# Fourteen of sixteen weight groups of an up projection as seven half-block products in place of eight

## The chip, the cores and the metric

The kernel runs on one core of a Trainium2 chip. The metric is the device time of one execution in microseconds. Before the change it is 2390.11 us, the median of 3 runs (2389.84 to 2390.34).

## What is computed

One layer of a decoder with a prompt group of 2048 tokens and a sample group of 64 tokens, model width 1024: an input projection, sliding-window attention and mLSTM heads, an output projection, then the channel MLP with hidden width 4096. The change is in the MLP alone:

```python
def channel_mlp(x, g, w_up, w_down):
    h = rmsnorm(x, g)
    u = jnp.maximum(jnp.einsum('btd,df->btf', h, w_up), 0)
    return jnp.einsum('btf,fd->btd', u * u, w_down)
```

All data are float32.

## The kernel before, in words

**Quarters.** The tokens are worked in four quarters of 512 (TQ); the last takes the 64 sample tokens too (576, TMAX). Each quarter runs weight units in a fixed order: 6 units F and 4 units T of the input projection (the attention and the mLSTM run between them), 4 units O of the output projection, and 32 units M of the MLP, from unit number U_M = 14 to UNITS - 1 = 45. An M unit is half a chunk: a chunk U is 512 hidden columns of w_up (two units of 256), a chunk D the same 512 rows of w_down (two units of 512 output columns). The order of chunks is U0, U1, D0, U2, D1, ... U7, D6, D7 (lines 160 to 162): two up units, two down units, and so on.

**Exactness by parts.** TensorE multiplies in a reduced float format (float32r), so each operand is kept as a high part and a low part (the rest), and each product is three matmuls: high x high, high x low, low x high (gemm, lines 2057 to 2069). High parts are made by ScalarE (a copy with rounding), low parts by VectorE (the source minus the high part). For weights these are split_act (ScalarE, line 702 with the norm's gain as a scale, line 705 without) and split_vec (VectorE, lines 1173 and 1177), from the pieces w_raw that SyncE loads (512 KB, three buffers); a unit has two pieces and there are two buffers of split weights, w_hi and w_lo.

**An up unit** is 2 tiles of 128 hidden columns, each over 8 blocks of 128 of the model width. The hidden column tile is the weight operand and the 512 tokens are the moving operand; in the last quarter the tokens go as 256 and 320. ScalarE takes relu out of PSUM (line 1055) and squares it rounded to the high part (line 1057); VectorE squares it and subtracts for the low part (line 1181). Up units use PSUM banks 0 to 3, down units banks 4 to 7, where VectorE adds each result to x1 (line 1181).

**Queues.** Every engine runs its own instructions in the order in which the code writes them, and waits on semaphores. In the MLP each engine walks the same units by a function step. The walks of ScalarE and VectorE prepare unit u + 1 during unit u.

**Around the ends.** Before the MLP, norm_tile scales a token tile, TensorE transposes it (turn), and high_tile and low_tile split it into a_hi and a_lo. The first unit's second half waits for all low parts. In the last down units of a quarter the next quarter's tokens are prepared: stats_ahead (ScalarE), scale_ahead (VectorE, lines 1515 to 1537) in units UNITS - 4 and UNITS - 2, turn_ahead (TensorE, transposes at line 2115, ahead of the unit's matmuls), high_ahead (ScalarE) and take_ahead (VectorE, line 1563) in units UNITS - 3 and UNITS - 1. In VectorE's step these calls stand ahead of the unit's own additions. TensorE's next quarter starts with a wait for all of take_ahead.

Of the kernel before, what the change touches and what calls it, by code (L numbers as in the profile page):

```python
# [6 lines left out]
F32 = mybir.dt.float32  # L7
# [7 lines left out]
P = 128  # L15
# [40 lines left out]
WMAX = KT * TMW  # L56

# [14 lines left out]


# [75 lines left out]

def up_order(u, NN):  # L150
# [7 lines left out]


MLP_HEAD = [("U", 0)]  # L160
MLP_BODY = 3
MLP_TAIL = [("U", NC - 1), ("D", NC - 2), ("D", NC - 1)]


def hymba_layer(nc, x_prompt, x_sample, cache_k_win, cache_v_win, state_C, state_n, state_m, rel_bias,
# [5 lines left out]
    with ctx:  # L171
        def sb(name, shape, dt=F32, where=ctx):
            return where.enter_context(nc.sbuf_tensor(name, shape, dt))


        raw = [sb(f"w_raw{s}", [P, WMAX // 2]) for s in range(RAW)]
        w_hi = [sb(f"w_hi{b}", [P, WMAX], F32R) for b in range(UNIT_BUFS)]
        w_lo = [sb(f"w_lo{b}", [P, WMAX], F32R) for b in range(UNIT_BUFS)]

# [3 lines left out]
        sample_parts, sample_again = slice(TQ, TMAX + NS), slice(TMAX, TMAX + NS)  # L183
        x1 = sb("x1", [P, BLK + 1, D])
        square = sb("square", [P, 4, P])
        ident, triu, ntriu, cmask = (square[:, i, :] for i in range(4))
        ones = sb("ones", [P, P], F32R)
        bias = sb("bias", [P, H, 2 * P])
# [4 lines left out]
        bgate = sb("bgate", [P, 2 * HM])  # L193
        kk = sb("kk", [P, 2, P + TMAX])
# [7 lines left out]
        kwin = bias[:, 0, 0:KVH * DH]  # L202
# [26 lines left out]
        oms = sb("oms", [NS, HM, DV], where=phase)  # L229
        phase.close()  # L230
# [3 lines left out]
        relu = sb("relu", [P, 2, TMAX], where=phase)  # L234
        usq = sb("usq", [P, 2, TMAX], where=phase)
# [34 lines left out]
        def signal(name, per, first=0, extra=0):  # L270
# [8 lines left out]
        w_high = signal("w_high", PIECES)  # L279
        w_split = signal("w_split", PIECES, RAW)  # L280
# [24 lines left out]
        up_out, up_read = signal("up_out", 4 * NC, 1), signal("up_read", 4 * NC, 1)  # L305
# [24 lines left out]
        (s_in, s_bias0, s_ck, s_msk, s_cs, s_rows, s_rowsok, s_rrows, s_cols, s_ccols, s_kout, s_kok, s_sout, s_nmax, s_sum,  # L330
         s_esa, s_esok, s_mout, s_ib, s_dadd, s_d, s_tout, s_k2, s_st, s_q, s_kw, s_h, s_hsq, s_hn, s_hout,
         s_p_ok, s_ptout, s_ptv, s_pta, s_o, s_os, s_on, s_osq, s_osum, s_oss, s_kwm, s_c, s_cok, s_new, s_res, s_nst,
         s_mix_vec, s_mix_act, s_split, s_nin, s_nout, s_ncopy, s_step) = (
            signal("s_" + n, 0) for n in (
                "in bias0 ck msk cs rows rowsok rrows cols ccols kout kok sout nmax sum "
                "esa esok mout ib dadd d tout k2 st q kw h hsq hn hout "
                "p_ok ptout ptv pta o os on osq osum oss kwm c cok new res nst "
                "mix_vec mix_act split nin nout ncopy step").split())
# [19 lines left out]
        def y_tile_last(j):  # L358

            return usq[:, :, :].rearrange("p a t -> p (a t)")[:, 0:D] if j == BLK else y_tile(j)  # L360
# [6 lines left out]
        def unit_shape(u):  # L367
            kind, i, w = unit_of(u)
            return (4, 512) if kind == "O" or kind == "M" and mlp_unit(i)[0] == "D" else (KT, w)

        def mlp_unit(m):

            order = MLP_HEAD + [(k, c) for i in range(MLP_BODY) for k, c in (("U", 2 * i + 1), ("D", 2 * i), ("U", 2 * i + 2), ("D", 2 * i + 1))] + MLP_TAIL
            kind, c = order[m // 2]
            return kind, c, m % 2

        chunk_parity = {}
        kinds = MLP_HEAD + [(k, c) for i in range(MLP_BODY) for k, c in (("U", 2 * i + 1), ("D", 2 * i), ("U", 2 * i + 2), ("D", 2 * i + 1))] + MLP_TAIL
        for n, (kind, c) in enumerate(kinds):
            chunk_parity[U_M + 2 * n] = chunk_parity[U_M + 2 * n + 1] = c % 2  # L380
# [2283 lines left out]
```

## Time and profile before

| | us |
|---|---|
| median of 3 runs | 2390.11 |
| span of the profiled execution | 2388.1 |
| TensorE busy (matmuls) | 2362.5 |
| TensorE weight loads busy | 2016.6 |
| VectorE busy | 1377.4 |
| ScalarE busy | 963.6 |
| GpSimd busy | 79.3 |

The span is the profiled execution from its first instruction to its last. Busy times are summed durations of an engine's instructions with overlaps counted once; weight loads run beside matmuls. A matmul's duration contains its way through the array, so the distance between the starts of two matmuls is shorter than the duration of one.

### The profile page before, as it was taken

How to read it: one execution, taken by the hardware profiler on the slowest of the kernel's cores; microseconds unless marked ns; L12 is line 12 of the kernel's file. 1: busy time of each engine (PE TensorE's matmuls, PEld its weight loads, DVE VectorE, ACT ScalarE, POOL GpSimd, SP SyncE). 2: the span in 40 equal slices, each digit the busy share in tenths (PEclk: the TensorE clock that was granted, in tenths of full speed). 3: DMA queues.
4: the chain of work that ended last, by engine and by line, in shares of the span. 5: the costliest groups of instructions: out<-in, count | busy, mean ns of one | idle time of the engine just before them, and what ended most of it. 6: DMA issues, size and time to landing. Idle time of an engine off the chain costs nothing.

```text
span 2388.1 us, 33521 instructions
## 1 busy us (share of the span) xinstructions
PE 2362.5 (99%) x13086; PEld 2016.6 (84%) x13086; DVE 1377.4 (58%) x3162; ACT 963.6 (40%) x2050; POOL 79.3 (3%) x136
## 2 busy tenths in 40 slices
PE   9999999999999999999999999999999999999998
PEld 8988888888897888888998788888888879889996
DVE  4478554456378654455456854554656785555555
ACT  4445433334345533334333543333434454333332
POOL 3000000000000000000000210000010000000000
PEclk9999999999999999999999999999999999999999
DMA  6212323333511223324421233223444122222221
GB/s 193 79 45 90 96 97 98 96 109 106 170 55 54 81 96 97 96 90 132 147 80 37 68 99 97 90 96 97 133 124 133 45 67 88 77 84 80 88 80 66
DMA packets 175402, 224.28 MB, mean 94 GB/s; under 512 B 15107, under 2 KB 126308, under 8 KB 175228
## 3 DMA queue, kind: packets, MB, share of 16 engines
q1 hardware_dynamic: 162636, 192.63, 25.8%
q10 hardware_dynamic: 6448, 19.40, 2.3%
q0 software_dynamic: 6160, 10.11, 1.6%
q8 instruction: 103, 1.69, 0.3%
q14 instruction: 55, 0.45, 0.1%
HBM read 210.72 MB, written 12.60 MB: 94 GB/s over the span
## 4 chain that ended last, share of the span: by engine, by line
PE 95%; DVE 4%; ACT 1%; issue 1%; DVEq 0%; ACTq 0%
PE ps L2066 28%; PE ps L2068 28%; PE ps L2067 27%; PE ps L2077 2%; PE ps L2207 2%; PE ps L2187 1%; PE ps L2196 1%; PE ps L2253 1%; PE ps L2256 1%; DVE w_lo L1177 1%; PE ps L2103 0%; PE ps L2596 0%; PE ps L2115 0%; PE ps L2232 0%; DVE w_lo L1173 0%
## 5 line engine op out<-in xcount | busy, mean ns | idle before, releaser
L2068 PE MATMUL ps<-a_hi,w_lo 128*128 128x512 f32 (+2 forms) x1672 | 583.9, 349 | 0.0
L2066 PE MATMUL ps<-a_hi,w_hi 128*128 128x512 f32 (+2 forms) x1672 | 582.1, 348 | 0.6 <-DVE a_lo L1181 0.2
L2067 PE MATMUL ps<-a_lo,w_hi 128*128 128x512 f32 (+2 forms) x1672 | 582.0, 348 | 0.0
L702 ACT ACTIVATE w_hi<-w_raw,gains 128x256 fp32r<-128x256 f32 (+1 forms) x576 | 253.2, 521 | 411.3 <-PE ps L2068 290.6
L2066 PE MATMUL ps<-w_hi,u_all 128*128 128x512 f32 x1024 | 403.8, 394 | 0.0
L2068 PE MATMUL ps<-w_hi,u_all 128*128 128x512 f32 x1024 | 403.8, 394 | 0.0
L2067 PE MATMUL ps<-w_lo,u_all 128*128 128x512 f32 x1024 | 401.3, 392 | 0.0
L2066 PEld LDWEIGHTS ps<-a_hi,w_hi 128*128 128x128 f32 x1672 | 315.8, 189 | 43.1 <-DVE a_lo L1181 1.4
L2067 PEld LDWEIGHTS ps<-a_lo,w_hi 128*128 128x128 f32 x1672 | 314.0, 188 | 40.9
L2068 PEld LDWEIGHTS ps<-a_hi,w_lo 128*128 128x128 f32 x1672 | 314.2, 188 | 39.4
L1181 DVE TENSOR_TENSOR x<-x,ps 128x512 f32<-128x512 f32 (+1 forms) x288 | 196.5, 686 | 259.8 <-PE ps L2068 241.9
L1177 DVE TENSOR_TENSOR w_lo<-w_raw,w_hi 128x1024 fp32r<-128x1024 f32 (+2 forms) x208 | 242.9, 1182 | 119.0 <-ACT w_hi L705 119.0
L1173 DVE SCALAR_TENSOR_TENSOR w_lo<-w_raw,gains,w_hi 128x256 fp32r<-128x256 f32 (+1 forms) x576 | 257.7, 510 | 58.0 <-ACT w_hi L702 58.0
L1181 DVE TENSOR_TENSOR usq<-relu 128x512 f32<-128x512 f32 (+2 forms) x160 | 95.8, 599 | 321.9 <-ACT relu L1055 321.1
L2066 PE MATMUL ps<-w_hi,a_hi 128*128 128x290 f32 (+1 forms) x768 | 262.0, 341 | 0.3 <-DVE w_lo L1177 0.3
L2067 PE MATMUL ps<-w_lo,a_hi 128*128 128x290 f32 (+1 forms) x768 | 252.7, 329 | 0.0
L2068 PE MATMUL ps<-w_hi,a_lo 128*128 128x290 f32 (+1 forms) x768 | 252.5, 329 | 0.0
L1055 ACT ACTIVATE relu<-ps 128x512 f32<-128x512 f32 (+2 forms) x160 | 83.4, 521 | 401.7 <-PE ps L2068 316.6
L705 ACT ACTIVATE w_hi<-w_raw 128x1024 fp32r<-128x1024 f32 (+2 forms) x208 | 201.7, 1017 | 106.7 <-PE ps L2068 75.7
L2068 PEld LDWEIGHTS ps<-w_hi,u_all 128*128 128x128 f32 x1024 | 192.2, 188 | 45.3
L2067 PEld LDWEIGHTS ps<-w_lo,u_all 128*128 128x128 f32 x1024 | 192.4, 188 | 44.7
L2066 PEld LDWEIGHTS ps<-w_hi,u_all 128*128 128x128 f32 x1024 | 192.2, 188 | 43.2
(378 smaller groups left out, 2336.1 us busy)
## 6 DMA issues: line engine op xcount, KB each, us to landing
w_raw<-in_w_up_dram SPq DMA_DIRECT2D x128, 512.0 KB, 3.7
w_raw<-in_w_down_dram SPq DMA_DIRECT2D x128, 512.0 KB, 3.5
w_raw<-in_w_out_dram SPq DMA_DIRECT2D x32, 512.0 KB, 3.5
w_raw<-in_w_in_dram SPq DMA_DIRECT2D x24, 580.0 KB, 4.9
w_raw<-in_w_in_dram SPq DMA_DIRECT2D x22, 512.0 KB, 3.7
w_raw<-in_w_in_dram SPq DMA_DIRECT2D x32, 256.0 KB, 2.9
wide<-in_x_prompt_dram ACTq DMA_DIRECT2D x12, 512.0 KB, 4.6
x<-in_x_prompt_dram ACTq DMA_DIRECT2D x9, 512.0 KB, 6.2
```

The costliest lines, as they stand in the source:

```text
L702: ins = eng.activation(w_hi[b][:, k * n:(k + 1) * n][:, s], src[:, s], ACT.Copy, scale=gain[:, a:a + 1])
L705: eng.activation(w_hi[b][:, k * n:(k + 1) * n], src[:, 0:n], ACT.Copy).then_inc(w_high.sem, 1)
L1055: eng.activation(relu[:, l % 2, 0:w], ps[(l + 2) % 4][:, 0:w], ACT.Relu).then_inc(up_read.sem, 1)
L1173: ins = eng.scalar_tensor_tensor(w_lo[b][:, k * n:(k + 1) * n][:, s], raw[raw_of(q, p)][:, s], gain[:, a:a + 1], w_hi[b][:, k * n:(k + 1) ...
L1177: eng.tensor_tensor(w_lo[b][:, k * n:(k + 1) * n], raw[raw_of(q, p)][:, 0:n], w_hi[b][:, k * n:(k + 1) * n].bitcast(F32), ALU.subtract).th ...
L1181: return eng.tensor_tensor(out, a, b, op)
L2066: eng.matmul(out, lh, rh, start=(k == ks[0]), stop=False)
L2067: eng.matmul(out, lh, rl, start=False, stop=False)
L2068: ins = eng.matmul(out, ll, rh, start=False, stop=(k == last))
L2077: ins = eng.matmul(out, lhs(k), right, start=(k == ks[0] and part == 0), stop=(k == ks[-1] and part == 1))
L2187: ins = eng.matmul(ps[b][:, at:at + 2 * P], zT[rs, h // 2, cs], kk[rs, int(g != par), j * P:j * P + 2 * P], start=True, stop=True)
L2207: ins = eng.matmul(values_at(g)[:, h, :], PT[:, 2 * g + half, h * P:(h + 1) * P], vv[:, j + half, g, :], start=(half == 0), stop=(half == 1))
```

## The change

The up projection of 14 of the 16 up units of each quarter (all but the first two) is computed by seven products. The unit's weights are cut into four blocks, by half of the model width (512 each) and by tile of 128 hidden columns; the tokens' activations into four blocks, by the same halves of the model width and by token half (256). With four sums of weight blocks (S1 to S4) and four sums of activation blocks (T1 to T4), seven products of a 128-column block over 512 give the four results by additions (Winograd's form of Strassen's scheme). Each product is still three matmuls per 128 of the width: 84 matmuls of 256 columns in place of 48 of 512. In the last quarter the 64 sample tokens ride with one token half, in four of the seven products.

- The activations' sums are made once per quarter (x_sums, 4 VectorE operations; then t_high_part on ScalarE and t_low_part on VectorE, four each). For them the normed activations are kept in float32: take_tile writes them from PSUM to SBUF times the norm's gain, and high_tile and low_tile read that. The gain is no longer in the weight splits.
- The weights' sums are made in each unit (sum_forms, 4 VectorE operations), then seven high parts (high_form, ScalarE) and seven low parts (low_form, VectorE), each 128x512, into a ring of nine slots in place of the two buffers; the plain M units use four slots each.
- The products stand in PSUM banks 0 to 3 in turn. ScalarE copies the first to SBUF (take_copy), VectorE adds the others up (take_sum 0 to 6). ScalarE then does relu, square and the rounding copy (square_up), VectorE the low part (low_sum).
- Buffers overlap otherwise, for room: the bias table of the attention lies where T parts lie in the MLP and is loaded again in every quarter (bias_again, GpSimd queue).
- The calls scale_ahead and take_ahead stand at the end of VectorE's step, behind the unit's additions.

The core of the diff:

```diff
+FORM = 512
+RING = 9
+N_PLAIN = 2
+FORMS_OF = "A11 A12 S1 S2 S4 S3 A22".split()
...
+        def ring_free(eng, q, u, f):
...
+            at = ring_at(u) + f
+            if at < RING:
+                eng.wait_ge(op_out.sem, op_out.at(q, op_end(NT, 2 if at < 4 else 3)))
+                return
+            v, g = RING_USER[at - RING]
+            kind, c, half = mlp_unit(v)
+            if seven(v) is not None:
+                eng.wait_ge(m_done.sem, m_done.at(q, 7 * seven(v) + g + 1))
+            elif kind == "U":
+                eng.wait_ge(up_out.sem, up_out.at(q, 2 * NN * (half + 1)))
+            else:
+                eng.wait_ge(dn_out.sem, dn_out.at(q, 2 * NT * c + NT * (half + 1)))
...
+        def product_bank(at, n):
+
+            return ps[(7 * at + n + 2) % 4]
```

On GpSimd's queue, and on ScalarE (step and its helpers):

```diff
+                if q < QI:
+                    pool.wait_ge(m_done.sem, m_done.at(q, 7 * N_SEVEN))
+                    bias_again()
...
+            def high_form(q, u, f):
+
+                name = FORMS_OF[f]
+                if name[0] == "S":
+                    eng.wait_ge(f_sum.sem, f_sum.at(q, 4 * seven(u) + {"S1": 1, "S3": 2, "S2": 3, "S4": 4}[name]))
+                else:
+                    landed(eng, q, 2 * u + int(name[2]) - 1)
+                ring_free(eng, q, u, f)
+                eng.activation(form_at(w_hi_all, u, f), form_src(q, u, name), ACT.Copy).then_inc(f_high.sem, 1)
...
+                def square_up(u, phi):
...
+                    eng.wait_ge(c_add.sem, c_add.at(q, 7 * at + 4 + 3 * phi))
+                    eng.activation(c_at[phi], c_at[phi], ACT.Relu).then_inc(u_rel.sem, 1)
+                    eng.wait_ge(u_rel.sem, u_rel.at(q, 2 * at + phi + 1))
+                    eng.activation(c_at[phi], c_at[phi], ACT.Square).then_inc(u_sq.sem, 1)
...
+                    eng.activation(u_hi[c % 2][:, half * 2 + phi, 0:T], c_at[phi], ACT.Copy).then_inc(u_high.sem, 1)
...
+                    if seven(u) is not None:
+                        if seven(u) == 0:
+                            t_high_part("T3")
+                        if before is not None:
+                            square_up(before, 1)
+                        take_copy(u)
+                        next_part(0)
+                        next_part(1)
+                        next_part(2)
+                        next_part(3)
+                        square_up(u, 0)
```

On VectorE:

```diff
+            def take_tile(q, NT, k):
...
+                    gain = gains[:, 2, 4 * m:4 * m + 4].unsqueeze(2).broadcast_to([P, 4, R])
+                    tt(x_flat(NT > BLK)[m][:, :, n * P:n * P + R], ps[4 + (2 * k + m) % 4][:, 0:4 * R].rearrange("p (k t) -> p k t", k=4), gain, ALU.mult).then_inc(xf_ok.sem, 1)
...
+                    if before is not None:
+                        take_sum(before, 6)
+                    if seven(u) is not None:
+                        if seven(u) == 0:
+                            t_low_part(3)
+                        next_part(0)
+                        if before is not None:
+                            low_sum(before, 0)
+                        next_part(1)
+                        take_sum(u, 0)
+                        if before is not None:
+                            low_sum(before, 1)
+                        next_part(2)
+                        take_sum(u, 1)
+                        take_sum(u, 2)
+                        next_part(3)
+                        take_sum(u, 3)
+                        next_part(4)
+                        take_sum(u, 4)
+                        take_sum(u, 5)
+                        next_part(5)
+                    elif kind == "U":
+                        if half:
+                            next_part(0)
+                            next_part(1)
+                            next_part(2)
+                        else:
+                            next_part(0)
+                            next_part(3)
+                            x_sums()
+                            t_low_part(0)
+                            t_low_part(1)
                         for n, (t, s) in enumerate(up_order(u, NN)):
...
+                            low_up(u, t, off, w, half * 2 * NN + n + 1)
...
+                        next_part(5)
+                    if u == UNITS - 4 and not last:
+                        scale_ahead(q + 1, 0)
+                    if u == UNITS - 3 and not last:
+                        take_ahead(q + 1, 0)
+                    if u == UNITS - 2 and not last:
+                        scale_ahead(q + 1, 1)
+                    if u == UNITS - 1 and not last:
+                        take_ahead(q + 1, 1)
```

Here next_part(0) and (1) are two weight sums each for the next unit, next_part(2) to (5) the low parts of forms 0 and 1, 2 and 3, 4, 5 and 6; for a plain next unit next_part(0) and (3) are its two splits. On TensorE:

```diff
+                    bank_free(0, 2)
+                    product(u, 0, ws, b11)
+                    bank_free(1, 4)
+                    product(u, 1, ws, b21)
+                    bank_free(2, 6)
...
+                    product(u, 2, ws, turned_part("T1"))
+                    bank_free(3, 7)
...
+                    product(u, 3, HT, turned_part("T2"))
+                    eng.wait_ge(cp_ok.sem, cp_ok.at(q, at + 1))
+                    product(u, 4, HT, b22)
+                    eng.wait_ge(c_add.sem, c_add.at(q, 7 * at + 1))
...
+                    product(u, 5, HT, turned_part("T3"))
+                    eng.wait_ge(c_add.sem, c_add.at(q, 7 * at + 3))
+                    product(u, 6, ws, turned_part("T4"))
```

bank_free(n, count) waits until VectorE has done that many takes of the unit before.

## Rows read from the trace of the kernel before

**Rows 1.** The page: span, then busy time of each engine, share, instructions.
```profile
span 2388.1 us, 33521 instructions
PE 2362.5 (99%) x13086; PEld 2016.6 (84%) x13086; DVE 1377.4 (58%) x3162; ACT 963.6 (40%) x2050; POOL 79.3 (3%) x136
```
**Rows 2.** Stage windows: us, busy of PE, PEld, DVE, ACT, POOL, clock, DMA.
```profile
238.00:594.00 356.00, 356.00 (x1558) 289.76 (x1557) 186.39 (x323) 137.07 (x262) 0.00 (x0) 1.00 0.32 101
...
1982.00:2366.00 384.00, 384.00 (x2286) 346.68 (x2285) 204.35 (x390) 130.44 (x274) 0.00 (x0) 1.00 0.25 79
```
**Rows 3.** Groups by line and shape, weight loads: busy, mean ns of one.
```profile
L2066 PEld LDWEIGHTS ps<-a_hi,w_hi 128*128 128x128 f32 x1672 | 315.8, 189 | 43.1 <-DVE a_lo L1181 1.4 <-DVE w_lo L1173 1.1 <-issue 1.0
```
**Rows 4.** Timeline of PE, 512 columns: start us, duration, instruction.
```profile
400.10 0.39 PE L2067 MATMUL ps<-a_lo,w_hi 128*128 128x512 f32 x1
...
404.27 0.39 PE L2067 MATMUL ps<-a_lo,w_hi 128*128 128x512 f32 x1
...
404.73 0.39 PE L2066 MATMUL ps<-w_hi,u_all 128*128 128x512 f32 x1
```
**Rows 5.** Timeline of PE, 256 columns, in two units.
```profile
1982.03 0.28 PE L2067 MATMUL ps<-a_lo,w_hi 128*128 128x256 f32 x1
...
1984.07 0.28 PE L2067 MATMUL ps<-a_lo,w_hi 128*128 128x256 f32 x1
...
2301.00 0.28 PE L2067 MATMUL ps<-a_lo,w_hi 128*128 128x256 f32 x1
...
2302.43 0.28 PE L2067 MATMUL ps<-a_lo,w_hi 128*128 128x256 f32 x1
```
**Rows 6.** Timeline of PE, 320 columns.
```profile
1979.89 0.31 PE L2067 MATMUL ps<-a_lo,w_hi 128*128 128x320 f32 x1
...
1981.62 0.31 PE L2067 MATMUL ps<-a_lo,w_hi 128*128 128x320 f32 x1
```
**Rows 7.** Groups by line and shape, DVE.
```profile
L1177 DVE TENSOR_TENSOR w_lo<-w_raw,w_hi 128x1024 fp32r<-128x1024 f32 x152 | 185.2, 1222 | 34.9 <-ACT w_hi L705 34.9
L1181 DVE TENSOR_TENSOR x<-x,ps 128x512 f32<-128x512 f32 x256 | 174.6, 686 | 242.4 <-PE ps L2068 241.9
...
L1181 DVE TENSOR_TENSOR ST<-ps,DT 128x256 f32<-128x256 f32 x32 | 12.1, 420 | 4.7 <-ACT DT L708 4.3
```
**Rows 8.** Timeline of DVE in an up unit.
```profile
400.78 0.69 DVE L1181 TENSOR_TENSOR u_all<-usq,u_all 128x512 fp32r<-128x512 f32 x1
401.38 1.22 DVE L1177 TENSOR_TENSOR w_lo<-w_raw,w_hi 128x1024 fp32r<-128x1024 f32 x1
```
**Rows 9.** Timeline of ACT behind an up unit.
```profile
404.93 0.60 ACT L1055 ACTIVATE relu<-ps 128x512 f32<-128x512 f32 x1 [4.26 <-PE ps L2068]
405.56 0.63 ACT L1057 ACTIVATE u_all<-relu 128x512 fp32r<-128x512 f32 x1
```
**Rows 10.** Timeline of DVE at the end of the first quarter.
```profile
566.61 0.17 DVE L1515 TENSOR_SCALAR st<-st 128x2 f32<-128x2 f32 x1 [2.00 <-ACT PT L793]
...
567.84 1.42 DVE L1537 TENSOR_SCALAR wide<-wide,st 128x1024 f32<-128x1024 f32 x2
...
576.45 4.23 DVE L1563 SCALAR_TENSOR_TENSOR a_lo<-ps,gains,a_hi 128x128 fp32r<-128x128 f32 x16 [0.75 <-ACT a_hi L837]
...
586.27 0.69 DVE L1181 TENSOR_TENSOR x<-x,ps 128x512 f32<-128x512 f32 x1 [2.11 <-PE ps L2068]
```
**Rows 11.** Timeline of PE there.
```profile
573.13 1.91 PE L2115 MATMUL ps<-square,wide 128*128 128x128 f32 x16
...
586.07 0.40 PE L2066 MATMUL ps<-a_hi,w_hi 128*128 128x512 f32 x1
```
**Rows 12.** Timeline of DVE at the start of the first MLP.
```profile
230.96 1.29 DVE L1181 TENSOR_TENSOR a_lo<-ps,a_hi 128x512 fp32r<-128x512 f32 x2 [0.86 <-ACT a_hi L735]
```
**Rows 13.** Timeline of PE there.
```profile
227.33 1.09 PE L2103 MATMUL ps<-square,wide 128*128 128x128 f32 x8 [0.63 <-DVE wide L1243]
...
232.31 0.39 PE L2066 MATMUL ps<-a_hi,w_hi 128*128 128x256 f32 x1
```

More of the change, by code:

```diff
@@ L71, in dmas_of, with mlp_unit, seven, plain_before @@
     return 3 if u == U_T else 1
+MLP_HEAD = [("U", 0)]
+MLP_BODY = 3
+MLP_TAIL = [("U", NC - 1), ("D", NC - 2), ("D", NC - 1)]
+MLP_ORDER = MLP_HEAD + [(k, c) for i in range(MLP_BODY) for k, c in (("U", 2 * i + 1), ("D", 2 * i), ("U", 2 * i + 2), ("D", 2 * i + 1))] + MLP_TAIL
+def mlp_unit(u):
+    kind, c = MLP_ORDER[(u - U_M) // 2]
+    return kind, c, (u - U_M) % 2
+def seven(u):
+    if not U_M <= u < UNITS:
+        return None
+    kind, c, half = mlp_unit(u)
+    return 2 * c + half - N_PLAIN if kind == "U" and 2 * c + half >= N_PLAIN else None
+N_SEVEN = sum(seven(u) is not None for u in range(UNITS))
+FORMS_OF = "A11 A12 S1 S2 S4 S3 A22".split()
+def plain_before(u):
+    return 2 * sum(seven(v) is None for v in range(u))
+PLAIN = plain_before(UNITS)
+def ring_at(u):
+    return sum(4 if seven(v) is None else 7 for v in range(U_M, u))
+RING_USER = [(u, f) for u in range(U_M, UNITS) for f in range(4 if seven(u) is None else 7)]
 def raw_of(q, p):
@@ L368, in unit_shape @@
             kind, i, w = unit_of(u)
[L369 to L380, printed above, removed]
+            return (4, 512) if kind == "O" or kind == "M" and mlp_unit(u)[0] == "D" else (KT, w)
         block = ctx.enter_context(nc.Block())
@@ L1988, in step @@
-                            eng.wait_ge(u_sq.sem, u_sq.at(q, o + 1))
-                            low(l, o, t, off, w)
-                            if n == NN - 1 and not end and u != U_M:
-                                split_vec(eng, nq, nu, 1, i)
+                            low_up(u, t, off, w, half * 2 * NN + n + 1)
+                        if half:
+                            for n in (3, 4, 5):
+                                next_part(n)
+                        else:
+                            t_low_part(2)
@@ L2561, in quarter, with t_at @@
                     eng.wait_ge(op_read.sem, op_read.at(q, 4 * NT))
-                def step(kind, c, half, u, i):
+                ws = staging(last)[0]
+                t_hi, t_lo = ({name: parts[i] for name, parts in t_forms(last).items()} for i in range(2))
+                def t_at(name, k, w):
+                    if name == "T2":
+                        return t_hi[name][:, k // 2, k % 2, 0:w], t_lo[name][:, k, 0:w]
+                    return t_hi[name][:, k, 0:w], t_lo[name][:, k, 0:w]
@@ new lines, in product @@
+                def product(u, f, w, right):
+                    eng.wait_ge(f_split.sem, f_split.at(q, 7 * seven(u) + f + 1))
+                    hi, lo = form_at(w_hi_all, u, f), form_at(w_lo_all, u, f)
+                    out = product_bank(seven(u), f)[:, 0:w]
+                    for k in range(4):
+                        rh, rl = right(k, w)
+                        eng.matmul(out, hi[:, k, :], rh, start=(k == 0), stop=False)
+                        eng.matmul(out, hi[:, k, :], rl, start=False, stop=False)
+                        ins = eng.matmul(out, lo[:, k, :], rh, start=False, stop=(k == 3))
+                    ins.then_inc(m_done.sem, 1)
```

641 lines of the change are left out of this document (444 added, 197 removed).

## The prediction

> **What bounds the kernel now.** I read the busy times of the page first: TensorE is busy 2362.5 of 2388.1 us, VectorE 1377.4, ScalarE 963.6 [rows 1]. Then the busy time by stage: in the MLP of the first quarter (238 to 594 us) TensorE is busy for all 356 us, VectorE for 186, ScalarE for 137; in that of the last quarter 384, 204 and 130 of 384 [rows 2]. So a matmul taken out there is time taken out, as long as the other two engines feed TensorE; VectorE has 170 us of room in a quarter's MLP. The granted clock is 1.00 in both stretches [rows 2], the upper level of 2.4 GHz, with TensorE never idle before; I leave the clock out of the sum.
>
> The duration of a matmul in the trace overlaps its neighbours, so I take its price from starts. At 512 columns, 18 matmuls from 400.10 to 404.27 us: 0.2317 us each [rows 4]. At 256 columns there are two rates: 18 from 1982.03 to 1984.07, 0.1133 each, and 12 from 2301.00 to 2302.43, 0.1192 each [rows 5]; in the last quarter they alternate from unit to unit. At 320 columns 12 from 1979.89 to 1981.62: 0.1442 [rows 6]. Each brings its own weight load, 189 ns long [rows 3], and the 256-column ones still start every 0.113 to 0.119 us, so loads are pipelined beside matmuls and half-width products cost half.
>
> The Trainium skill (TensorE: Matmul & The Clock Gate, Back-to-back issue gap) gives 262 cycles for 256 columns and 518 for 512, but adds that spacing in a stream is set by weight load and matmul together. By its isolated figures a plain unit would be 48 x 0.216 = 10.4 us and seven products 84 x 0.109 = 9.2, an estimate that saves 1.2 us where the rows below save 1.36; its warning about the load would speak against 84 small matmuls, but the starts of rows 5 show no such cost.
>
> **What TensorE saves.** A plain unit (256 hidden columns) is 2 tiles x 8 k x 3 passes = 48 matmuls of 512 columns, 11.12 us. Seven products are 7 x 4 k x 3 = 84 matmuls of 256 columns: 9.52 us at the fast rate, 10.01 at the slow one. The new weight slots lie elsewhere in memory, so I can't tell which; I take the middle, 0.1162, or 9.76 us. It saves 1.36 us (1.11 to 1.60), times 14 units times 3 quarters: 57.1 us (46.6 to 67.2). In the last quarter a plain unit is 48 of 256 and 48 of 320 columns, 5.58 + 6.92 = 12.50 us; four of its seven products stay 320 wide and three are 256: 6.92 + 36 x 0.1162 = 11.10. It saves 1.40 (1.2 to 1.5), times 14: 19.6 us. **Together 76.7 us, 64 to 88.**
>
> **What VectorE and ScalarE must do for it.** To prepare one seven-unit, VectorE makes 4 sums and 7 low parts of 128x512; to finish one it takes 7 partial sums of 128x256 out of PSUM and makes 2 low parts of 128x512. A 128x512 operation lasts 686 ns, a 128x256 one 420, a 128x1024 one 1222 [rows 7], but one that depends on nothing just before starts 0.60 us after a 128x512 one (400.78 to 401.38 [rows 8]); so 0.60, about 0.33 (420 less the same 90) and 1.13. ScalarE's steps are 0.60 and 0.63 [rows 9]; each reader of PSUM starts 0.20 us after the next group's first matmul (404.73 to 404.93 [rows 4, 9]).
>
> The units go up, up, down, down. In a first up unit (start 0, end 9.76) VectorE comes out of the down unit late: last addition at 0.2, two low parts whose slots came free only when that unit ended, done at 2.0. Then 4 sums (4.5), first take (4.9), two low parts (6.1), second and third take (6.9), two low parts (8.1), fourth (8.4), a low part (9.0), fifth and sixth (9.7), two low parts (10.9), seventh (11.3). TensorE's seventh product, at 8.4, must wait for the third take: ready by 1.5 us. The second unit's first four products, at 9.8, 11.2, 12.5 and 13.9, need takes done at 6.9, 8.4, 9.7 and 11.3. The second up unit has for VectorE only two 128x1024 splits, 7 takes, 2 low parts, 5.9 us. ScalarE has 7 high parts at about 0.5 (an estimate from those rows, less the overlap), a copy and 6 dependent steps of 0.66, about 8 of 9.76 us. I cost the steady state at nothing; if the takes were over 1.5 us later, each further us would be a us of TensorE in each of 28 pairs.
>
> The Trainium skill (VectorE: DVE Perf Modes, The TRN2 errata) says that every instruction that reads SBUF pays a fixed extra time, so many small ones are dear; its formula (N+151)/0.96 gives 691 ns for 512 elements, which is the row's 686 for one alone, but rows 8 show that 90 ns of it overlap the next. By the full durations the third take would come near 8.2, still before 8.4.
>
> **The start of each MLP.** Three additions. (a) The norm's tiles now go PSUM, VectorE (times the gain), ScalarE, VectorE, where it was PSUM, ScalarE, VectorE. TensorE already idles there: 0.63 us for VectorE's norm, and it starts its second half at 232.31 right behind the low parts of 230.96 [rows 12, 13]. Two more 128x512 operations for each of four tiles, against gains that leave the weight splits: I estimate 1.7 us more. (b) In the two plain units VectorE gets 4 sums of activations and 3 low parts, all 128x1024 (8 us), besides 11 form operations. Counted from the end of the norm, the forms' third low part is 0.65 us late, because VectorE's order puts the second plain output before it and ScalarE squares that one in three steps after the unit's end. (c) In the first seven-unit, a 128x1024 low part and the 4 sums of the next unit stand ahead of the first take, which the sixth product needs: 2.1 us late, and the seventh product 0.6 more. Together 1.7 + 0.65 + 2.1 + 0.6 = 5.1 us, times 4: **20 us** (8, if most is hidden, to 32).
>
> **The end of each quarter but the last.** In the kernel before, VectorE's next-quarter work stands ahead of the additions of a down unit; the change puts it behind them. VectorE runs in order, so it now begins only when TensorE has finished that down unit. The additions behind a unit end 0.8 us after it (start 586.27, 0.20 after TensorE went on at 586.07, and 0.60 of work [rows 10, 11]). The scaling for the transposes runs from 566.61 to its first tile, begun at 567.84 [rows 10]: 1.23, plus 0.7 for that tile. TensorE's 16 transposes (573.13, 1.91 us long [rows 11]) stand ahead of the next down unit and so start 2.8 us late, in two units: 5.7 us. The low parts of the last two tiles take 4.23 us (576.45 [rows 10]); TensorE's next quarter waits for all of them before its first matmul: 0.2 + 0.6 + 4.2 + 0.1 = 5.1 us where there was no gap at 586.07. That is 10.8 us, three times: **32 us** (25 to 38; 0 only if something else let VectorE pass, and it is in order). The bias table is loaded again in each quarter, 8 loads beside two down chunks (44 us) and the next projections; I cost it at nothing; uncovered it would be tens of us.
>
> **The sum.** 2388.1 - 76.7 + 20 + 32 = 2363.4 us of span; the median of the runs stands 2.0 us above this profile's span, so 2365.4, call it 2366 us, 1.0% less.
>
> **The rivals.** (A) Most of the waits are hidden or shorter, and the gain comes through: 76.7 less some 10: 2390 - 67 = 2323 us. For: VectorE's 170 us of room [rows 2]. Against: it is order, not room, that makes the waits. 12%. (B) The other side: the bank handover in the seven-units decides. A product needs the bank of the one four before it; where VectorE gets to its third take after 8.4 us, TensorE stops. The price is what it is late, 28 times; the gain of 24 us is gone at 0.86 us per pair, that is takes 2.4 us later than my schedule. With takes 3 us later, 1.5 us of stall per pair: 42 us, 2408. For: the first unit's VectorE work (8.9 us, 10 by full durations) is as long as TensorE's 9.76, and every take is behind waits on ScalarE. Against: the second unit has 4 us to catch up. 11%. (C) A mild form of it, or 256-column matmuls all at the slow rate and dearer starts: within 5 us of before, 2388. 7%. (D) It doesn't do what it says: a half-width matmul limited by its 189 ns load would make a seven-unit 15.9 us, 2390 + 56 x 4.7 = 2650; rows 5 exclude it. 1%.
>
> **How the numbers follow.** My own case has 69%, with 2348 to 2383 from its terms. The range 2332 to 2388 takes in half of A's surroundings and most of C, and leaves out about 2 in 10. What a measurement tells from no change is about 0.2%, 5 us. Faster: mine and A, 82%; within 0.2%: C, 7%; slower: B and D, 11%.
>
> **What would show it.** Right: in 56 units, 84 matmuls starting every 0.113 to 0.119 us; up units of 9.5 to 10 us without gaps in the steady state; at each quarter's end two gaps near 2.8 us ahead of the transposes, waiting for VectorE's scaling, and one near 5 us ahead of the next projection, behind the low parts of a_lo; gaps of 2 and 0.6 us in the first seven-unit. Wrong: gaps in every seventh product (B), no gaps at the quarters' ends (A), or starts further apart than 0.12 us.

## The result and the profile after

| | before, same chip | changed kernel |
|---|---|---|
| median of 4 runs | 2390.23 us | 2410.64 us |
| lowest to highest | 2389.84 to 2390.92 | 2405.98 to 2411.23 |
| span of the profiled execution | 2388.1 us | 2409.4 us |
| mean granted clock of TensorE in it | 0.999 | 0.990 |

The change makes the kernel 0.81% slower: ratio 1.0081, 95% interval 1.0067 to 1.0095. The prediction was 2366 us, with a range of 2332 to 2388; sign, value and range were all wrong. The busy times of the page, to be held against [rows 1]:

```profile
span 2409.4 us, 37391 instructions
PE 2321.0 (96%) x14430; PEld 2051.5 (85%) x14430; DVE 1654.1 (69%) x3597; ACT 1116.5 (46%) x2110; POOL 92.3 (4%) x161
```

TensorE is busy 41.5 us less than before and idle 88.4 us (2409.4 less 2321.0) where it was idle 25.6. So the products are cheaper, and what they save is lost beside them. The windows of the first quarter's MLP and of its parts (us; busy of PE, PEld, DVE, ACT, POOL; clock; DMA) tell where:

```profile
238.00:594.00 356.00, 341.16 (x2062) 302.79 (x2061) 252.49 (x440) 176.54 (x298) 4.38 (x8) 0.99 0.32 103
...
223.00:240.00 17.00, 13.22 (x92) 12.21 (x91) 15.12 (x29) 8.53 (x15) 0.00 (x0) 0.91 0.25 77
...
545.00:574.00 29.00, 24.76 (x115) 19.84 (x113) 17.30 (x41) 11.28 (x29) 0.00 (x0) 1.00 0.39 129
574.00:590.00 16.00, 14.54 (x64) 12.11 (x64) 6.30 (x10) 5.87 (x19) 0.00 (x0) 0.89 0.18 49
590.00:600.00 10.00, 5.35 (x15) 4.26 (x16) 9.49 (x27) 6.53 (x11) 0.00 (x0) 0.66 0.26 72
600.00:620.00 20.00, 20.00 (x89) 16.25 (x88) 4.47 (x5) 3.79 (x7) 0.00 (x0) 1.00 0.70 253
```

The MLP that had TensorE busy for all of 238 to 594 [rows 2] now has 341.16 us. The losses sit at its two ends, and in three of these stretches the granted clock is below 1.

**The end of the quarter.** Three gaps were predicted (2.8, 2.8, 5.1 us). In the timeline of PE (start us, duration, instruction; in brackets the idle time before it and its releaser) the second and the third are:

```profile
572.13 0.40 PE L2478 MATMUL ps<-w_hi,u_all 128*128 128x512 f32 x1
...
575.20 3.43 PE L2529 MATMUL ps<-square,wide 128*128 128x128 f32 x16 [2.67 <-DVE wide L1825]
...
589.34 0.40 PE L2478 MATMUL ps<-w_hi,u_all 128*128 128x512 f32 x1
594.65 0.79 PE L2476 MATMUL ps<-a_hi,w_hi 128*128 128x512 f32 x1 [4.92 <-DVE a_lo L1851]
595.25 0.63 PE L2477 MATMUL ps<-a_lo,w_hi 128*128 128x512 f32 x1
595.67 0.63 PE L2478 MATMUL ps<-a_hi,w_lo 128*128 128x512 f32 x1
```

By starts, less one normal spacing, they are 2.84 and 5.08 us, and the one at 545.25 is 2.93: 10.85 in sum against 10.8. Each stands behind the instruction that the prediction named; in the timeline of VectorE the last addition of the down unit, and behind it the low parts of a_lo:

```profile
572.57 0.69 DVE L1461 TENSOR_TENSOR x<-x,ps 128x512 f32<-128x512 f32 x1 [2.08 <-PE ps L2478]
...
574.39 1.42 DVE L1825 TENSOR_SCALAR wide<-wide,st 128x1024 f32<-128x1024 f32 x2
...
589.77 0.69 DVE L1461 TENSOR_TENSOR x<-x,ps 128x512 f32<-128x512 f32 x1 [2.09 <-PE ps L2478]
590.38 4.22 DVE L1851 SCALAR_TENSOR_TENSOR a_lo<-ps,gains,a_hi 128x128 fp32r<-128x128 f32 x16
```

What was not predicted follows the gap. The transposes take 3.43 us (1.91 before [rows 11]), and after the third gap matmuls of 512 columns start 0.43 us apart (595.25 to 595.67) until 598.66, where they were 0.2317 apart [rows 4]: the lower clock level, 1.2 of 2.4 GHz, for some 4 us. With the lower clock the end of the first quarter costs 14.1 us. In the second the same three gaps (1118.56, 1148.34, 1165.74) cost 17.4, since there the clock falls behind the first of them too.

**The steady state.** In the timeline of VectorE, a second up unit, the one ahead of two down units:

```profile
355.45 0.42 DVE L1461 TENSOR_TENSOR wide<-wide,ps 128x256 f32<-128x256 f32 x1
359.12 1.23 DVE L1422 TENSOR_TENSOR w_lo<-w_raw,w_hi 128x1024 fp32r<-128x1024 f32 x1 [3.25 <-ACT w_hi L839]
360.26 0.68 DVE L1461 TENSOR_TENSOR u_all<-wide,u_all 128x512 fp32r<-128x512 f32 x1
361.08 0.42 DVE L1461 TENSOR_TENSOR wide<-ps,wide 128x256 f32<-128x256 f32 x1
```

VectorE idles 3.25 us for the high part of the next down unit's weights, with its first take queued behind. ScalarE makes that part only after six steps of its own, and on TensorE the sixth product waits for the take (0.47 - 0.12 = 0.35 us by starts):

```profile
357.23 0.63 ACT L1231 ACTIVATE u_all<-wide 128x512 fp32r<-128x512 f32 x1
...
358.04 2.00 ACT L839 ACTIVATE w_hi<-w_raw 128x1024 fp32r<-128x1024 f32 x2
```

```profile
361.09 0.28 PE L2995 MATMUL ps<-a_hi,w_lo 128*128 128x256 f32 x1
361.56 0.39 PE L2993 MATMUL ps<-a_hi,w_hi 128*128 128x256 f32 x1 [0.19 <-DVE wide L1461]
```

This stands in every pair of units of the first three quarters; in the second pair it is 0.51 us, in the first 1.30 to 1.40. The group by lines adds it up with the waits of the first seven-unit, all of it behind VectorE (busy, mean ns | idle before and its releaser):

```profile
L2993 PE MATMUL ps<-a_hi,w_hi 128*128 128x256 f32 (+1 forms) x896 | 257.6, 288 | 14.6 <-DVE wide L1461 14.6
```

And the product itself is dearer than the middle rate taken. In one unit, first and last start of the first, second and third product:

```profile
386.71 0.28 PE L2993 MATMUL ps<-a_hi,w_hi 128*128 128x256 f32 x1
...
388.01 0.28 PE L2995 MATMUL ps<-a_hi,w_lo 128*128 128x256 f32 x1
388.13 0.28 PE L2993 MATMUL ps<-a_hi,w_hi 128*128 128x256 f32 x1
...
389.45 0.28 PE L2995 MATMUL ps<-a_hi,w_lo 128*128 128x256 f32 x1
389.56 0.28 PE L2993 MATMUL ps<-t_all,w_hi 128*128 128x256 f32 x1
...
390.81 0.28 PE L2995 MATMUL ps<-t_all,w_lo 128*128 128x256 f32 x1
```

That is 0.118 and 0.120 us (1.30 and 1.32 over 11 spacings) and, for the third product, which reads t_all, 0.114. Of the seven products of the steady pairs six run at 0.118 to 0.120 and this one at 0.113 to 0.114; a pair of units takes 20.30 us where two plain ones took 22.24.

**The start of the MLP.** In the first unit of all (timeline of PE) TensorE ends its first half and waits for a_lo; then the clock falls again:

```profile
233.85 0.28 PE L2478 MATMUL ps<-a_hi,w_lo 128*128 128x256 f32 x1
236.11 0.38 PE L2476 MATMUL ps<-a_hi,w_hi 128*128 128x256 f32 x1 [1.99 <-DVE a_lo L1461]
...
237.99 0.41 PE L2478 MATMUL ps<-a_hi,w_lo 128*128 128x256 f32 x1
```

A gap of 2.15 us that was 0.31, and then 0.21 us per matmul for some 3 us in place of 0.119. In the timeline of VectorE, the two lines L1461 with x_all are the added work, two operations in 1.28 us each, and the low parts wait behind them:

```profile
230.79 1.28 DVE L1461 TENSOR_TENSOR x_all<-ps,gains 128x512 f32<-128x512 f32 x2
232.17 1.29 DVE L1461 TENSOR_TENSOR a_lo<-x_all,a_hi 128x512 fp32r<-128x512 f32 x2
233.38 1.28 DVE L1461 TENSOR_TENSOR x_all<-ps,gains 128x512 f32<-128x512 f32 x2
234.76 1.29 DVE L1461 TENSOR_TENSOR a_lo<-x_all,a_hi 128x512 fp32r<-128x512 f32 x2
```

Another gap, of 1.33 us, stands ahead of this unit (behind 223.99), where the kernel before has 0.10. It ends with VectorE's split of the unit's second piece of weights, and the same added work is ahead of that: x_all of the tile before (221.33), then ScalarE's a_hi of that tile and its high part of the weights, done at 224.24, then the split:

```profile
221.33 1.28 DVE L1461 TENSOR_TENSOR x_all<-ps,gains 128x512 f32<-128x512 f32 x2
...
224.27 1.23 DVE L1422 TENSOR_TENSOR w_lo<-w_raw,w_hi 128x1024 fp32r<-128x1024 f32 x1 [0.26 <-ACT w_hi L839]
```

In the second quarter the same gap of 2.15 us (behind 808.57) brings no lower clock; the window behind it:

```profile
812.00:816.00 4.00, 4.00 (x36) 4.00 (x35) 3.97 (x5) 1.06 (x1) 0.00 (x0) 1.00 0.63 169
```

In the first seven-unit the gaps are 0.75, 1.98 and 0.46 us; 0.65, 2.1 and 0.6 were predicted.

### The profile page after: what moved, and what is told of

It reads as the page before. It is cut to its first block, busy times and chain, and to the rows that moved or that the text cites. A ratio compares the mean times of both kernels' runs of the same rounds, so it can differ in the third digit from the quotient of the medians.

```text
span 2409.4 us, 37391 instructions
## 1 busy us (share of the span) xinstructions
PE 2321.0 (96%) x14430; PEld 2051.5 (85%) x14430; DVE 1654.1 (69%) x3597; ACT 1116.5 (46%) x2110; POOL 92.3 (4%) x161
## 4 chain that ended last, share of the span: by engine, by line
PE 74%; DVE 18%; ACT 5%; issue 3%; DVEq 0%; ACTq 0%
PE ps L2476 18%; PE ps L2478 18%; PE ps L2477 18%; DVE w_lo L1461 5%; PE ps L2993 3%; PE ps L2994 3%; PE ps L2995 3%; DVE wide L1461 2%; PE ps L2487 2%; PE ps L2621 2%; DVE PT L1461 2%; DVE w_lo L1422 2%; PE ps L2601 1%; ACT w_hi L839 1%; DVE a_lo L1461 1%
## 5 line engine op out<-in xcount | busy, mean ns | idle before, releaser
L1461 DVE TENSOR_TENSOR x<-x,ps 128x512 f32<-128x512 f32 (+1 forms) x288 | 197.2, 685 | 184.8 <-PE ps L2478 167.0
L1422 DVE TENSOR_TENSOR w_lo<-w_raw,w_hi 128x1024 fp32r<-128x1024 f32 (+1 forms) x160 | 176.7, 1115 | 205.9 <-ACT w_hi L839 205.8
L2993 PE MATMUL ps<-a_hi,w_hi 128*128 128x256 f32 (+1 forms) x896 | 257.6, 288 | 14.6 <-DVE wide L1461 14.6
L2994 PE MATMUL ps<-a_lo,w_hi 128*128 128x256 f32 (+1 forms) x896 | 255.7, 285 | 0.0
L2995 PE MATMUL ps<-a_hi,w_lo 128*128 128x256 f32 (+1 forms) x896 | 255.0, 285 | 0.0
L2476 PE MATMUL ps<-a_hi,w_hi 128*128 128x512 f32 (+2 forms) x552 | 192.3, 348 | 26.8 <-DVE a_lo L1851 14.8
L2478 PE MATMUL ps<-a_hi,w_lo 128*128 128x512 f32 (+2 forms) x552 | 190.0, 344 | 0.0
L2477 PE MATMUL ps<-a_lo,w_hi 128*128 128x512 f32 (+2 forms) x552 | 189.6, 343 | 0.0
L2993 PEld LDWEIGHTS ps<-a_hi,w_hi 128*128 128x128 f32 x896 | 169.1, 189 | 21.0 <-DVE wide L1461 19.9
L2994 PEld LDWEIGHTS ps<-a_lo,w_hi 128*128 128x128 f32 x896 | 169.0, 189 | 1.2
L2995 PEld LDWEIGHTS ps<-a_hi,w_lo 128*128 128x128 f32 x896 | 169.3, 189 | 0.0
```

What stands on the lines that cost most here:

```text
L1422: ins = eng.tensor_tensor(w_lo_all[:, to:to + b - a], src[:, a:b], w_hi_all[:, to:to + b - a].bitcast(F32), ALU.subtract)
L1461: return eng.tensor_tensor(out, a, b, op)
L2476: eng.matmul(out, lh, rh, start=(k == ks[0]), stop=False)
L2477: eng.matmul(out, lh, rl, start=False, stop=False)
L2478: ins = eng.matmul(out, ll, rh, start=False, stop=(k == last))
L2993: eng.matmul(out, hi[:, k, :], rh, start=(k == 0), stop=False)
```

## Where the 45 us between prediction and result lie

From the starts of matmuls in both traces, in us; saved is negative:

| first quarter | predicted | measured |
|---|---|---|
| six steady pairs of seven-units | -16.3 | -11.5 |
| first pair | +0.6 | +2.6 |
| head of the MLP: gaps | +1.7 | +3.1 |
| head: lower clock behind them | 0 | +1.5 |
| end of quarter: three gaps | +10.8 | +10.85 |
| end of quarter: lower clock | 0 | +3.3 |
| together | -3.2 | +9.8 |

The predicted +0.6 of the first pair is its 0.65, 2.1 and 0.6 less the 2.7 that it saves. Read at the same matmul of the next quarter in both traces (the first with Mline at 158.44, 723.39, 1305.45 and 1892.23 us before; 159.13, 733.84, 1327.77 and 1923.48 after), the four quarters give +9.8, +11.9, +8.9 and -9.9 us, where -3.2 three times and -14.5 were predicted. The second quarter has the most lower clock (6.5 us in place of 4.8), the third some 4, of which 1.5 (1807.1 to 1810.5) stand behind no gap. The differences and 0.7 us ahead of them come to 21.3 us, that of the spans; a sum predicted at -24 leaves 45 us to explain.

## The experiments

All but one take the changed kernel and undo or move one thing, the last several; one takes the kernel before. The kernel before was run beside them: 2390.3 us beside the order, take-first and padding kernels, 2390.5 beside the others.

**Order of the next quarter's work on VectorE.** The calls go back to where the kernel before had them, the seven products stay.

```diff
                         next_part(1)
+                        if u == UNITS - 4 and not last:
+                            scale_ahead(q + 1, 0)
...
+                        if u == UNITS - 1 and not last:
+                            take_ahead(q + 1, 1)
                         for n, (j, R) in enumerate(down_tiles(last, u)):
...
-                    if u == UNITS - 4 and not last:
-                        scale_ahead(q + 1, 0)
...
-                    if u == UNITS - 1 and not last:
-                        take_ahead(q + 1, 1)
```

> The changed kernel with VectorE's four preparations of the next quarter (scale_ahead, take_ahead) put back ahead of the additions of their down units. Theory 'order': the gaps of 2.9, 2.8 and 5.1 us at the end of each of three quarters come from VectorE reaching the preparations only behind the last addition; they shrink to about 1.6 (the statistics of the first two tiles are ready only at 545.1 us), 0 and 0, and the TensorE clock, which fell after such gaps, stays at 1.00 there, 3 us more per quarter. Sum 12 us a quarter: 2410.6 - 37 = 2373 us. Rival 'late data': the preparations wait for their loads and for ScalarE anyway; then the gaps stay where they are, 2405 to 2411.

2376.74 us (2372.32 to 2377.1), ratio 0.9941, interval 0.9925 to 0.9958: 34 us less than the changed kernel, and now faster than before. The second and third gap of each quarter are gone. Where 585 to 600 us held a gap and half clock, its windows show:

```profile
574.00:585.00 11.00, 11.00 (x49) 8.93 (x48) 8.06 (x21) 4.29 (x12) 0.00 (x0) 1.00 0.25 70
585.00:600.00 15.00, 15.00 (x67) 12.22 (x66) 7.61 (x12) 5.93 (x12) 0.00 (x0) 1.00 0.61 211
```

Here, without the gap, the clock stays at 1.00, so the low stretch of the changed kernel came with the gap. At the first pair of next-quarter tiles gaps of 1.87 us (ahead of the transposes) and 1.72 us (ahead of the next down unit) stay in the first quarter, 1.2 and 1.7 in the second and third. They stand behind ScalarE's statistics, whose tile had not landed:

```profile
541.08 1.06 ACT L960 ACTIVATE t_plain<-PT 128x1024 f32<-128x1024 f32 x1 [1.00 <-DMA PT<-in_x_prompt_dram]
```

So of the 32.6 us of gaps 9.4 are left and 23 gone; the rest is lower clock (0.997 in the mean of this profile, 0.990 in that of the changed kernel). Not all of that belongs to the order: behind the first head, whose gap of 2.15 us is unchanged, the clock did not fall in this profile (1.00 from 233 to 240).

**The same order in the kernel before.** The same eight lines moved behind the loop of additions in the kernel before; every up unit stays plain.

> The kernel before (eight products) with one part of the change alone: scale_ahead and take_ahead behind the additions of their down units. Theory 'order': three gaps of about 2.8, 2.8 and 5.1 us at each of three quarter ends, 32 us, and 2 to 4 us a quarter for the clock that falls after them: 2390.2 + 32 + 9 = 2431 us (2422 to 2435). Rival 'late data' (the gaps of the changed kernel come from its other loads and sums): 2390 to 2396.

2437.07 us (2435.77 to 2437.73), ratio 1.0192 (1.0177 to 1.0208). The order alone costs 46.8 us, without one product of seven. Its timeline of PE shows the gaps of the changed kernel to the hundredth, and long transposes too, 3.63 us:

```profile
580.66 3.63 PE L2115 MATMUL ps<-square,wide 128*128 128x128 f32 x16 [2.67 <-DVE wide L1537]
...
600.41 0.79 PE L2066 MATMUL ps<-a_hi,w_hi 128*128 128x512 f32 x1 [4.92 <-DVE a_lo L1563]
```

**Earlier loads of those tiles.** On top of the first experiment, ScalarE issues the two loads ahead of its squares of that unit instead of behind them.

```diff
                         next_part(3)
+                        if u == UNITS - 5 and not last:
+                            load_ahead(q + 1, 0)
+                            load_ahead(q + 1, 1)
                         square_up(u, 0)
```

> The kernel with the preparations ahead of the additions (2376.7 us), and the loads of the next quarter's first two token tiles moved ahead of ScalarE's last square of that unit. In the run before, two gaps of 1.9 and 1.7 us stayed at each quarter's last but one down chunk, because the statistics of these tiles came late. Theory: they wait for ScalarE's place in its queue to issue the load; issued 4 to 5 us earlier, the gaps go, with 1 us of slow clock: 3 quarters x 4 = 10 to 13 us less, 2365. Rival: the load is late because it shares the DMA queues with the reload of the bias table (248 GB/s there); then at most a third of it goes, 2373.

2369.8 us (2367.09 to 2370.09), ratio 0.991 (0.9896 to 0.9925): 6.9 us less than the first experiment, 5 short of what was expected. Of the two gaps one of 0.68 us is left in the first quarter and one of 0.66 in the others, so 7.4 of the 9.4 us are gone: the theory of the late issue holds and the rival (a third at most) fails, but the gaps were smaller than the 4 us a quarter that the expectation took.

**The take ahead of the next down unit's split.** In the steady state, VectorE's split that waits for ScalarE goes behind the first take.

```diff
-                        next_part(0)
+                        if seven(nu) is not None:
+                            next_part(0)
                         if before is not None:
                             low_sum(before, 0)
                         next_part(1)
                         take_sum(u, 0)
+                        if seven(nu) is None:
+                            next_part(0)
```

> The changed kernel with one edit on VectorE: in the second up unit of a pair, the split of the next down unit's weights stands behind the first take instead of ahead of it. Theory: VectorE waits there 3.25 us for ScalarE's high parts, and the first take comes 0.35 us too late for the sixth product; the gap of 0.35 us in each pair goes: about 24 pairs, 8 us, 2402. Rival: the take waits for ScalarE's copy of the first product anyway (it stands behind ScalarE's square), and the gap stays: 2411.

2397.55 us (2395.52 to 2400.39), ratio 1.0031 (1.0019 to 1.0043): 13 us less than the changed kernel, where 8 to 9 were expected. The same group by lines:

```profile
L2996 PE MATMUL ps<-a_hi,w_hi 128*128 128x256 f32 (+1 forms) x896 | 255.8, 285 | 6.7 <-DVE wide L1461 6.7
```

Idle time before products falls from 14.6 to 6.7 us, and 0.35 us is gone from every pair. The trace counts as idle only 0.19 of each 0.35, since the first matmul behind a gap is recorded longer (0.39 against 0.28). By starts the gaps of all seven-units fall from 23.0 to 11.4 us. The matmul behind such a gap also takes 0.11 us more to the next start (0.23 against 0.12), some 2.5 us for 23 waits; the two together account for the 13.

**The first pair.** In the first seven-unit three takes go ahead of the sums for the next unit.

```diff
-                        next_part(0)
+                        if seven(u):
+                            next_part(0)
...
-                        next_part(1)
+                        if seven(u):
+                            next_part(1)
...
-                        next_part(2)
+                        if seven(u):
+                            next_part(2)
...
                         take_sum(u, 2)
+                        if seven(u) == 0:
+                            next_part(0)
+                            next_part(1)
+                            next_part(2)
```

> The changed kernel with one edit on VectorE in the first seven-unit of each quarter: the first three takes stand ahead of the four weight sums and two low parts for the next unit. Theory: the gaps of 2.0 and 0.46 us before its sixth and seventh products go, and the next unit's forms come 0.7 us late instead: 4 x 1.8 = 7 us less, 2403. Rival: VectorE has too much work there in any order, and the gap only moves to the second unit: 2411.

2409.25 us (2405.95 to 2412.48), ratio 1.0075 (1.0058 to 1.0092): 1.4 us less than the changed kernel, within its spread. The gaps 1.98, 0.46 and 1.30 become 0.60, 0.54, 0.69 and 1.83, and the first pair and the plain units before it take 46.90 us against 46.93. What is done later is awaited later: VectorE's work there is too much for this order and for the old one. My theory was wrong here, the rival right.

**Where the weights lie.** 64 bytes of padding per partition between the low weights and a_hi.

```diff
         w_hi_all, w_lo_all = sb("w_hi", [P, UNIT_BUFS * WMAX], F32R), sb("w_lo", [P, UNIT_BUFS * WMAX], F32R)
+        sb("pad", [P, 16])
```

> The changed kernel with 64 bytes of nothing between w_lo and a_hi, so that all tensors but the weights lie 64 bytes further. Theory 'placement': 256-column matmuls start every 0.113 us when weights and moving data differ by 64 modulo 128 bytes, and every 0.118 to 0.119 when they do not. Products 1, 2, 5 and 6 (moving data in a_hi and a_lo) go from 0.119 to 0.1133, product 3 (T1) from 0.1134 to 0.119, 4 and 7 stay: 12 us less, 2399. Rival 'traffic' (the rate is set by what VectorE, ScalarE and the loads do beside it): the rates by product stay as they are, 2411.

2408.68 us (2407.2 to 2410.46), ratio 1.0075 (1.006 to 1.009). The third product, fast until now, becomes slow:

```profile
385.65 0.28 PE L2994 MATMUL ps<-t_all,w_hi 128*128 128x256 f32 x1
...
386.98 0.28 PE L2996 MATMUL ps<-t_all,w_lo 128*128 128x256 f32 x1
```

1.33 us over 11 spacings, 0.121 against 0.114, and in the steady pairs none of the others becomes fast. So the place of a tensor in SBUF does bear on the spacing, but the rule that I had formed (that the distance of weights and activations modulo 128 bytes decides for all seven) is wrong. Nor is place all of it. In the first quarter's first seven-unit (251.39) the padded kernel runs its first, second and fifth product at 0.1145, 0.1127 and 0.1145, where the changed kernel has 0.120, 0.119 and 0.119; in the third quarter the first two of these are back at 0.119. And in the changed kernel, without any padding, the third product of the second seven-unit runs at 0.119 in the first quarter (270.85) and at 0.113 and 0.114 in the second and third (844.10, 1439.18), with the same instructions in the same slots. The rival 'traffic' is thus refuted for the steady pairs only.

**The ring of weights moved whole.** One raw buffer ahead of the weight ring and the others behind it, which shifts the weights against everything else.

```diff
-        raw = [sb(f"w_raw{s}", [P, WMAX // 2]) for s in range(RAW)]
+        raw = [sb("w_raw0", [P, WMAX // 2])]
         w_hi_all, w_lo_all = sb("w_hi", [P, UNIT_BUFS * WMAX], F32R), sb("w_lo", [P, UNIT_BUFS * WMAX], F32R)
+        raw += [sb(f"w_raw{s}", [P, WMAX // 2]) for s in range(1, RAW)]
```

> The changed kernel with the weights' ring at other addresses (w_raw1 and w_raw2 behind it; all else where it was), so that weights and a_hi, a_lo have the residues modulo 128 bytes (32 and 96) of the fast units of the kernel before. Theory 'placement': the products with moving data in a_hi and a_lo (1, 2, 5, 6) start every 0.1133 us and not 0.119, T1's go from 0.1134 to 0.119: 12 us less, 2398. Rival: the rate isn't set by these residues; the rates by product stay near 0.119 or shuffle, 2405 to 2415.

2407.16 us (2406.31 to 2408.26), ratio 1.007 (1.0055 to 1.0085). The 12 us that the theory promised did not come. In the first unit of the steady pairs (the mean of 18 units) all seven products have the spacings of the padded kernel to within 0.0002 us (0.1187, 0.1190, 0.1209, 0.1183, 0.1194, 0.1189, 0.1182). Two layouts with the same shift of the weights against the activations, by different means, give the same rates there, so relative place counts. It doesn't fix the rate alone: in the second quarter's second seven-unit the first two products run at 0.113 in this layout and at 0.119 in the padded one. What the full rule is stays open; no layout made all seven fast, and at 0.1133 throughout a seven-unit would take 9.5 us.

**All of what helped.** The order, the early loads, the take first, and the takes of the first pair.

> The changed kernel with the four edits of order together: preparations ahead of the additions, early load of the next tiles, split behind the first take in the second unit of a pair, takes ahead of the sums in the first seven-unit. If they are independent the savings add: 2410.6 - 34 - 10 - 13 - 7 = 2347 us. If they overlap (each frees the same time of VectorE, or the clock comes back only once), 2355 to 2365. Either is faster than the kernel before (2390.2), which says that seven products pay once VectorE's order doesn't stop TensorE.

2353.38 us (2353.11 to 2353.81), ratio 0.9844 (0.983 to 0.9859): 37 us faster than the kernel before and 57 faster than the changed one, with the same products. The single steps add up: 40.8 for order and loads, 13.1 and 1.4 make 55.3. The takes of the first pair add nothing that can be seen: that pair takes 23.62 us here and 23.67 in the take-first kernel. Its windows of the first quarter's end:

```profile
545.00:590.00 45.00, 45.00 (x205) 36.89 (x204) 30.89 (x67) 19.66 (x45) 0.00 (x0) 1.00 0.40 123
590.00:600.00 10.00, 10.00 (x45) 8.10 (x44) 2.17 (x3) 2.28 (x5) 0.00 (x0) 1.00 1.01 368
```

A steady pair takes 19.84 us, 0.1181 per matmul, without gaps. What it still leaves is the head (gaps of 1.32, 0.79 and 2.14 us, of which the 0.79 is in the kernel before too; lower clock from 235.3 to 238.5) and the first pair.

## Why the prediction was wrong

- **End of the quarters: the mechanism and the gaps right, the price too small.** 10.85 us of gaps against 10.8, behind the instructions named. The step "I leave the clock out of the sum" failed. It was read from stretches in which TensorE never idled [rows 2], and then used for stretches in which I had myself put gaps of 3 to 5 us. Behind them the clock ran at its lower level: 3.3 us lost in the first quarter, and at the quarters' ends gone where the gaps are gone (first experiment). The order alone cost 46.8 us in the kernel before, against the 32 in the sum.
- **"I cost the steady state at nothing": wrong.** Two parts. The schedule for VectorE counted its work and its waits for TensorE, and for the first unit of a pair it held: takes at 349.1, 350.7 and so on, no gap. For the second unit I added up 5.9 us of work and concluded that there was room; there the order is what binds. The split of the next down unit stands ahead of the takes and waits 3.25 us for a ScalarE whose eight us of work I had counted but never set in order against VectorE's. That is rival B in kind, small in size: 0.35 us (about 0.46 with the slower restart) per pair in place of its 1.5, and 1.30 in the first pair. That its 2408 lies near the 2410.6 measured is luck. Taking the wait away gave 13 us.
- **The price of a matmul: the term of 76.7 us was mis-sized.** 0.1181 us in place of the middle rate of 0.1162; a steady pair without gaps saves 2.40 us in place of 2.72, so some 2.2 us per quarter. It lay inside the bounds of the term (64 to 88), nearer the lower. With the waits the pair saved 1.94.
- **Head of the MLP: one gap right, one missing.** 1.7 us was the estimate for two more operations on each of four tiles. Four of them, of 0.6 us, stand on VectorE ahead of the second half, and the gap there grew by 1.84 us. That the same operations delay the split of the unit's own weights (1.23 us more ahead of the unit) was not in the sum, nor were the 1.5 us of lower clock.
- **First pair: right where a wait was followed, wrong in one.** 0.75, 1.98 and 0.46 us against 0.65, 2.1 and 0.6. The 1.30 is the wait of the steady state again.
- **Bias at nothing: right.** Its 32 loads of 128 KB take 5.3 us each from issue to landing, and no gap of TensorE stands behind them.

The misses nearly all have one sign, and so they add: of some 45 us about 15 are clock (4.8, 6.5 and 4 us), 13 the waits on ScalarE (2.8 and 1.4 us a quarter, and in the last less), 8 the rate, 6 the gaps of the heads (1.4 us each), and some 3 are not assigned. The range was built from independent terms and had no term for the clock. The chances were also added wrongly: 69 and 12% for a faster kernel are 81, and 11 and 1% for a slower one 12.

Open: the rule of placement behind 0.113 or 0.119 us, and how much of the head could be won; no kernel changed the head by itself. What the clock does behind a given gap is open too.

## What to carry to other kernels

Write down the order of each in-order engine with its waits on every other engine, not only its sum of work: here both costly waits stood in queues with room to spare. A gap on a saturated TensorE can cost more than its length, since the granted clock may fall behind it: here some 14 us on top of 41 us of gaps (three times 10.85, and 2.15 in each of four heads). When a change saves on one engine and loses elsewhere, move the lost part alone into the kernel before: the eight moved lines cost 46.8 us there, and putting them back made a slower kernel a faster one.

## What was unexpected of the hardware

- In the steady pairs the spacing of 256-column matmuls depends on where weights and moving data lie relative to each other in SBUF: 0.113 to 0.114 or 0.121 us for the same product, moved by 64 bytes of padding, and reproduced by another layout with the same relative shift. In a quarter's first two seven-units it was 0.113 or 0.119 at one and the same place, so something else bears on it too.
- The clock did not fall behind every gap, and equal gaps differed. Behind 2.15 us in the first head TensorE ran 0.8 us at full rate and then at half (236.93 to 240.1), in the second head not at all; the same gap of the first head left the clock at 1.00 in the first experiment; behind 2.93 us it stayed up in the first quarter (545 to 574 at 1.00) and fell to 0.50 in the second; behind 2.84 us it fell in the first two quarters and not in the third (1740 to 1746 at 1.00); behind 5.08 us it was down from the first matmul on, in all three quarters:

```profile
1118.00:1123.00 5.00, 2.23 (x11) 1.75 (x10) 4.24 (x11) 2.25 (x4) 0.00 (x0) 0.80 0.32 113
1123.00:1127.00 4.00, 4.00 (x17) 3.61 (x16) 0.38 (x1) 4.00 (x16) 0.00 (x0) 0.50 0.54 143
...
1170.00:1174.00 4.00, 2.95 (x14) 2.95 (x15) 3.62 (x9) 3.02 (x7) 0.00 (x0) 0.50 0.17 33
...
1761.00:1766.00 5.00, 4.44 (x11) 3.49 (x12) 2.85 (x5) 2.52 (x6) 0.00 (x0) 0.50 0.51 135
```

(Windows of the changed kernel, columns as above.) No experiment changed a gap's length while keeping the rest, so what decides stays open.

- The clock also fell once without a gap. In the last quarter's projections of the changed kernel (in the sum above, in the third stretch), behind small matmuls of the sample tokens' attention and mLSTM, TensorE was busy 6.94 of 7 us at 1.00 and then ran at half for 3 us; in the kernel with all edits the same stands from 1750.7 to 1754.1:

```profile
1800.00:1807.00 7.00, 6.94 (x103) 5.71 (x103) 3.94 (x14) 1.75 (x3) 0.00 (x0) 1.00 0.67 161
1807.00:1810.00 3.00, 3.00 (x9) 2.35 (x8) 0.55 (x3) 0.00 (x0) 1.24 (x2) 0.51 0.41 109
```
